# Moving the step sizes of a state-space mixer ahead of a branch, reordering its last group, and filling four waits with unread products

## What is computed

```python
def hgrn2_mixer(h, lb, w_in, o_norm, w_o):            # 8 heads
    ...
    o = rms_norm(o, o_norm) * gate
    return o.reshape(B, S, HV).astype(h.dtype) @ w_o

def ssd_mixer(z, xbc, dt, conv_w, conv_b, dt_bias, a_log, d_skip, norm_g):
    xbc = jax.nn.silu(causal_conv(xbc, conv_w, conv_b))
    ...
    dtc = jax.nn.softplus(dt.astype(jnp.float32) + dt_bias)   # 32 heads, in 4 groups of 8
    a = -jnp.exp(a_log)
    a_cum = jnp.cumsum(dtc * a, axis=2)                       # within chunks of 128 tokens
    ...
    y = rms_norm_2(y * jax.nn.silu(z), norm_g)

def second_block(x, ...):
    h = rms_norm_2(x, norm1_g[l])
    u = h @ w_in[l]                                           # dt is 32 of its columns
    ...
    mix = (gates[:, :, 0] * (y_a @ w_br_dsa[l]) + gates[:, :, 1] * (y_b @ w_br_nsa[l])
           + gates[:, :, 2] * (y_c @ w_br_ssd[l]))
    x = x + mix @ w_out[l]
    h = rms_norm_2(x, norm2_g[l])
    x = x + jnp.square(jax.nn.relu(h @ w_ff1[l])) @ w_ff2[l]
```

## Time and profile before

| | us |
|---|---|
| median of 3 runs | 2938.66 (2938.01 to 2939.58) |
| the profiled execution | 2933.7 |
| its span | 2931.9 |
| TensorE busy | 2760.3 (94%) |
| VectorE busy | 1620.9 (55%) |
| ScalarE busy | 1139.9 (39%) |
| GpSimd busy | 121.8 (4%) |

### The profile page before, as it was taken

How to read it: one execution, slowest core, us unless ns; L and a number is a source line. 1 busy time by engine, 2 the same in 40 slices (tenths; PEclk the granted TensorE clock), 3 DMA queues, 4 the chain that set the end, 5 groups by cost and what they waited for, 6 DMA issues and landing times.

```text
span 2931.9 us, 39152 instructions
## 1 busy us (share of the span) xinstructions
PE 2760.3 (94%) x14079; PEld 2226.9 (76%) x14079; DVE 1620.9 (55%) x3030; ACT 1139.9 (39%) x1896; POOL 121.8 (4%) x106
## 2 busy tenths in 40 slices
PE   7999999999999999998998998999899989999998
PEld 5567888888888788887675885667777767778887
DVE  6335726456554662645755347754677765464452
ACT  4344322236553422223437325842255543232221
POOL 0000000000000000000230001000011110000000
PEclk9999999999999999998999989999899999999999
DMA  4112333312111233232120220012222222333331
GB/s 142 38 58 72 115 93 94 100 44 79 57 57 36 79 115 93 94 100 65 58 72 1 87 70 18 1 56 81 74 70 72 65 65 72 115 101 101 93 100 65
DMA packets 59685, 217.83 MB, mean 74 GB/s; under 512 B 6433, under 2 KB 6561, under 8 KB 59425
## 3 DMA queue, kind: packets, MB, share of 16 engines
q1 hardware_dynamic: 57920, 209.76, 23.0%
q0 software_dynamic: 1632, 6.29, 0.6%
HBM read 211.83 MB, written 4.19 MB: 74 GB/s over the span
## 4 chain that ended last, share of the span: by engine, by line
PE 79%; DVE 11%; ACT 4%; issue 3%; DVEq 2%; ACTq 0%; DMA 0%; POOL 0%; SPq 0%
PE ps L366 22%; PE ps L368 22%; PE ps L367 22%; DVE work L2088 1%; PE ps L506 1%; DVE big L3176 1%; DVEq L3229 1%; DVE ring_lo L306 1%; PE ps L757 1%; PE ps L1558 1%; DVE work L2107 1%; PE ps L2014 1%; ACT ring_hi L299 1%; PE ps L1843 1%; PE ps L567 1%
## 5 line engine op out<-in xcount | busy, mean ns | idle before, releaser
L366 PE MATMUL ps<-a_hi,ring_hi 128*128 128x512 f32 (+1 forms) x1984 | 787.5, 397 | 45.1 <-DVE ring_lo L306 26.2
L368 PE MATMUL ps<-a_hi,ring_lo 128*128 128x512 f32 (+1 forms) x1984 | 772.7, 389 | 0.0
L367 PE MATMUL ps<-a_lo,ring_hi 128*128 128x512 f32 (+1 forms) x1920 | 746.2, 389 | 0.0
L306 DVE TENSOR_TENSOR ring_lo<-ring,ring_hi 128x1024 fp32r<-128x1024 f32 x358 | 437.9, 1225 | 518.5 <-ACT ring_hi L299 488.7
L299 ACT ACTIVATE ring_hi<-ring 128x1024 fp32r<-128x1024 f32 x378 | 397.6, 1055 | 507.9 <-PE ps L368 505.6
L366 PEld LDWEIGHTS ps<-a_hi,ring_hi 128*128 128x128 f32 x1984 | 379.8, 191 | 128.9 <-issue 21.3
L368 PEld LDWEIGHTS ps<-a_hi,ring_lo 128*128 128x128 f32 x1984 | 378.7, 191 | 77.7
L367 PEld LDWEIGHTS ps<-a_lo,ring_hi 128*128 128x128 f32 x1920 | 367.3, 191 | 71.2 <-issue 1.2
L367 PE MATMUL ps<-hid_lo,ring_hi 128*128 128x512 f32 (+1 forms) x992 | 381.1, 384 | 0.0
L366 PE MATMUL ps<-hid_hi,ring_hi 128*128 128x512 f32 (+1 forms) x928 | 354.6, 382 | 1.5 <-DVE ring_lo L306 1.5
L368 PE MATMUL ps<-hid_hi,ring_lo 128*128 128x512 f32 (+1 forms) x928 | 354.3, 382 | 0.0
(11 more groups left out here) (411 smaller groups left out, 3350.7 us busy)
## 6 DMA issues: line engine op xcount, KB each, us to landing
ring<-weights SPq DMA_DIRECT2D x392, 512.0 KB, 3.6
h<-x SPq DMA_DIRECT2D x1, 2048.0 KB, 9.5
residual<-h POOLq DMA_DIRECT2D x4, 512.0 KB, 3.5
h<-residual POOLq DMA_DIRECT2D x1, 2048.0 KB, 11.1
out<-h POOLq DMA_DIRECT2D x1, 2048.0 KB, 7.8
tab<-tables SPq DMA_DIRECT2D x1, 1648.0 KB, 15.8
big<-positions SPq DMA_DIRECT2D x1, 256.0 KB, 3.7
col<-columns SPq DMA_DIRECT2D x1, 164.5 KB, 3.9
```

The costliest lines, as they stand in the source:

```text
L306: dve.tensor_tensor(lo, M.ring[:, b % RING, :], hi.bitcast(F32), ALU.subtract).then_inc(M.sem("blocks_split"), 1)
L366: pe.matmul(out, w_hi, hi, start=start, stop=False)
L367: pe.matmul(out, w_hi, lo, start=False, stop=False)
L368: return pe.matmul(out, w_lo, hi, start=False, stop=stop)
```

## The change

1. `hgrn_pe`: `total` is called at k=6 instead of k=4.
2. `Pairs.pe`: six products that nobody reads between the first and the second scores.
3. dt gets a stage of its own, `ssd_dt`, one block, between the pairs of nsa and `nsa_out`. Its product goes to a PSUM bank of its own (`STEP_BANK`). VectorE's series is cut in four parts, one in each turn of `nsa_out`, between the first two rests and the first sum; ScalarE's exponentials stand before `nsa_out` and behind its first turn. The second block of `nsa_out` is rounded and its rest made among the splits of y. The loops of ScalarE and VectorE in `branch_out_*` are written out; TensorE's stays a loop. `ssd_pe` begins with `project(0, 0)`.
4. Last group of ssd: VectorE makes the last head's differences right after the ones before, and both last products with `cb` before the third pair's output; the rest of a block, two sums and the four `low` come behind. ScalarE has the last head's exponentials a step earlier. Four unread products stand before the last `output`, four at the start of `ssd_out_pe`.
5. `tail_pe`: the first two blocks of `mix_out` run over seven of eight steps as soon as `mix_split` has seven, then over the eighth; the other six follow.
6. The first block of `ff_up0` has places of its own (`first_hi`, `first_lo`) and is rounded and split during `mix_out`.

The same weights are loaded in the same number of blocks; nothing else is moved on SP's or GpSimd's queues.

```diff
-    ("nsa_in", 18), ("dsa_out", 8), ("nsa_out", 16),
-    ("ssd_in", 41), ("ssd_gate", 8), ("ssd_out", 16), ("mix_out", 8),
+    ("nsa_in", 18), ("dsa_out", 8), ("ssd_dt", 1), ("nsa_out", 16),
+    ("ssd_in", 40), ("ssd_gate", 8), ("ssd_out", 16), ("mix_out", 8),
...
+    if b == FIRST["ff_up0"]:
+        return M.first_hi[:, :], M.first_lo[:, :], RING
...
-            if k == 4 and between:
+            if k == (4 if j else 6) and between:
                 between()
...
         scores(0, 0)
+        idle_pe(pe, M, PIECE_BANK, 6)
         scores(0, 1)
...
-    with dve.Fori(0, NT // 2) as i:
+    for i in range(NT // 2):
         for u in range(2):
             rest_block(dve, M, FIRST[name] + u + 2, i, 4)
+        beside(i)
         for u in range(2):
             dve.wait_ge(M.sem("gates_ready"), i * 2 + (u + 1 + NT * BRANCHES.index(name)))
...
     R.pairs.pe(pe, M, compressed)
+
+    b = FIRST["ssd_dt"]
+    wait_split(pe, M, b)
+    for k in range(BLK):
+        mm = split_matmul(pe, M, M.bank(STEP_BANK), b, k, M.a_hi[:, k, :], M.a2_lo[:, k, :], k == 0, k == 7)
+    mm.then_inc(used, 1)
     branch_of_pairs_pe(pe, M, "nsa", NT)
...
-    branch_out_act(act, M, "nsa_out")
+    steps_logs_act(act, M, ssd)
+    round_block(act, M, FIRST["nsa_out"] + 1)
+    branch_out_act(act, M, "nsa_out", lambda i: steps_exp_act(act, M, ssd) if i == 0 else None)
...
-    branch_out_dve(dve, M, "nsa_out", lambda: split_y_dve(dve, M, "nsa", R.y))
+
+    def before():
+        split_y_dve(dve, M, "nsa", R.y, range(0, 5))
+        rest_block(dve, M, FIRST["nsa_out"] + 1)
+        split_y_dve(dve, M, "nsa", R.y, range(5, NT))
+
+    branch_out_dve(dve, M, "nsa_out", before, lambda i: steps_dve(dve, M, ssd, i))
...
     pe.wait_ge(M.sem("nsa_out_free"), NT + 2)
-    project(0, -1)
     for s in range(2):
         project(0, s)
...
             if s == 9:
+                if g + 1 == GRPS:
+                    idle_pe(pe, M, 0, 4)
                 output(g, 3)
...
     pe.wait_ge(M.sem("ssd_free"), SSD_READ + NT)
+    idle_pe(pe, M, 0, 4)
...
+def steps_dve(dve, M, R, part):
...
+    if part == 1:
+        dve.wait_ge(M.sem("small_done"), 6)
+        dve.tensor_scalar(t_, ab, 2.0, None, ALU.add)
+        dve.drain()
+        dve.reciprocal(s_, t_)
...
+        series((15, 13))
+    if part == 2:
+        series((11, 9, 7, 5, 3))
...
+    last = GRPS - 1
+    mix(last, 7)
+    segments(last, 7)
+    decay_cb(last, 6)
+    decay_cb(last, 7)
+    pair_out(last, 2)
+    rest_block(dve, M, FIRST["ssd_gate"] + NT + 1)
+    sums(7)
+    low(range(0, 4))
+    pair_out(last, 3)
+    sums(9)
...
-    pe.wait_ge(M.sem("ssd_out_free"), NT + 2)
+
+    pe.wait_ge(M.sem("ssd_out_free"), NT + 1)
+    pe.wait_ge(M.sem("mix_split"), NT - 1)
+    for u in range(2):
+        part_of_tile_pe(pe, M, "mix_out", u, M.in_hi, M.in_lo, range(0, NT - 1))
     pe.wait_ge(M.sem("mix_split"), NT)
-    gemm_split_pe(pe, M, "mix_out", NT, 1, lambda k: M.in_hi[:, k, :], lambda k: M.in_lo[:, k, :], 4)
+    for u in range(2):
+        part_of_tile_pe(pe, M, "mix_out", u, M.in_hi, M.in_lo, range(NT - 1, NT))
+    gemm_split_pe(pe, M, "mix_out", NT, 1, lambda k: M.in_hi[:, k, :], lambda k: M.in_lo[:, k, :], 4, done=2,
+                  looped=False)
...
+        else:
+            act.wait_ge(M.sem("blocks_used"), FIRST["mix_out"])
+            round_block(act, M, FIRST["ff_up0"], fresh=True)
         tile(t)
     act.wait_ge(M.sem("blocks_used"), FIRST["ff_up0"])
-    round_block(act, M, FIRST["ff_up0"], fresh=True)
     round_block(act, M, FIRST["ff_up0"] + 1, fresh=True)
```

More of the change, by code:

```diff
@@ L2124 @@
 BRANCHES = ["nsa_out", "ssd_out"]
+STEP_BANK = 4
 def branch_out_pe(pe, M, name, y_hi, y_lo, wait_y):
@@ L2143, in branch_out_pe, with branch_out_act @@
             mm.then_inc(used, 1)
-def branch_out_act(act, M, name):
-    with act.Fori(0, NT // 2) as i:
+def branch_out_act(act, M, name, behind):
+    for i in range(NT // 2):
         for u in range(2):
@@ L2154, in branch_out_act, with branch_out_dve @@
             round_block(act, M, FIRST[name] + u + 4, i, 4)
-def branch_out_dve(dve, M, name, before):
+        behind(i)
+def branch_out_dve(dve, M, name, before, beside):
     dve.drain().then_inc(M.sem(f"{name}_free"), 2)
     before()
-    with dve.Fori(0, NT // 2) as i:
+    for i in range(NT // 2):
         for u in range(2):
             rest_block(dve, M, FIRST[name] + u + 2, i, 4)
+        beside(i)
         for u in range(2):
@@ L3123, in ssd_act @@
         for s in range(STEPS):
-            if s != 1:
+            if s != 1 and not (g + 1 == GRPS and s == 8):
                 mix(g, s)
+            if g + 1 == GRPS and s == 7:
+                mix(g, 8)
             if g + 1 < GRPS:
@@ L3307, in ssd_dve @@
     for g in range(GRPS):
-        for s in range(STEPS):
+        for s in range(STEPS if g + 1 < GRPS else NT - 1):
             if s == 1:
@@ L3313, in ssd_dve @@
             if s == 9:
-                if g + 1 == GRPS:
-                    low(range(0, 4))
                 pair_out(g, 3)
@@ L3621, in lay_weights @@
     z, sx = w["sz"], w["sx"]
-    order = [wide(w["sdt"])]
+    put("ssd_dt", pack(wide(w["sdt"])))
+    order = []
     for g in range(GRPS):
```

157 lines of the change are left out of this document (79 added, 78 removed).

## The result

| | before | changed |
|---|---|---|
| median, us | 2939.12 (2938.01 to 2941.74, 4 runs) | 2896.29 (2895.42 to 2902.01, 4 runs) |
| profiled execution | 2933.7 | 2896.5 |
| its span | 2931.9 | 2894.7 |
| mean granted clock in it | 0.972 | 0.980 |

The ratio is 0.9857, interval 0.9840 to 0.9874; the change gains 42.8 us. The prediction was 2910.8 us, a gain of 27.9, with a range that began at 2901: right in sign, too small by a third, and the time lies outside the range. Between the two profiled executions the gain is 37.2 us.

A forecast was written before the change was run, and what follows sets the result against it. TensorE, busy 94% of the span, was taken to bound the kernel. 7.8 + 1.0 + 13.0 + 2.7 + 2.4 + 1.0 = 27.9 us off the 2938.66 median gave 2910.8 us, range 2901 to 2921.

The forecast's parts named there:

- the two new waits: Third turn of `nsa_out`, 3.0 us plus 1.6 of clock; `mix_out` before its third block, 2.0 us plus 1.4.
- the series: VectorE's step-size work inside `nsa_out`: hidden but for 3.0 us, where without cover it would cost some 17.
- the unread products of the last group: Before the last `output` and before `ssd_out`: worth nothing and costing nothing.
- the footing on the median: Whole kernel: the median of 2938.66 us is 5.0 above the profiled execution, and the gain was taken off that median.
- the heads: Recurrent heads: six waits of 1.30 us before the total go, 7.8 us; bounds 6.5 and 7.8.
- the pairs: Second scores in `Pairs.pe`: six idle products take 1.46 us and the clock falls later, 1.0 us; bounds 0 and 3.7.
- terms 5 and 6: `mix_out` begun early, 2.4 us (bounds 2.2 and 3.9); `ff_up0`'s first block rounded early, 1.0 us (0.8 and 2.4).
- Rival a: Pairs, `nsa_out`, `mix_out`, `ff_up0`: the clock stays at 2.4 GHz, together 7 us more won, 2904 us; chance 0.20.
- the bound of 3.7: Second scores in `Pairs.pe`: 2.2 + 1.5 us would go if the clock stood.
- Step sizes: `ssd_dt` moved ahead of `nsa_out`: 17.6 less 3.0 of waiting and 1.6 of clock, 13.0 us; bounds 11 and 16.
- Last group: Last group of ssd: the new order fills VectorE's own waits, 2.7 us; bounds 1.5 and 3.4.

The follow-up runs named there:

- run 4: The changed kernel with three calls of unread products in the pairs instead of six: 2896.49 us.
- Runs 1 and 2: The kernel before with one edit each: the heads' total at k=6 instead of k=4, 2924.79 us; two calls of unread products before each total's wait, 2928.84 us.
- run 9: The changed kernel itself once more, with no further edit: 2895.37 us, ratio 0.9860.

## Why the prediction was wrong

**The direction** was right: each of the six terms is a gain at its place, the two new waits came where forecast (2.27 us for 3.0, 1.88 for 2.0), the series is hidden but for 2.27 us, the unread products of the last group are worth nothing. The sum was too small by 14.9 us, and the steps that failed are, by size: the footing on the median (5.6), the heads, where the clock behind the waits was put at nothing (5.1), and the pairs, where the unread products were miscounted (3.6). The clock behind the two waits of terms 5 and 6 adds 2.4.

The likeliest case was not the one that came. Rival a, "the clock is kept", came for the pairs, `nsa_out` and `mix_out` and by less than half for `ff_up0`, and was itself too small: it said 2904. That it came owes something to luck. At the pairs it needed twelve passes and not the six of the prediction, after which the clock falls (run 4); and the same waits in `nsa_out` and before `mix_out`'s third block were followed by 1.2 GHz in the half-filled kernel.

**1. Heads, 12.9 instead of 7.8.** The failed step is "six waits of 1.30 us, so 7.8 us go". Only the waits were priced; the clock behind them stood at nothing, with no row for it. The nearest row was the gap of 1.81 us that isn't followed by the lower clock, and the granted clock of the heads was never asked for. Runs 1 and 2 show the missing 5.1 as three stretches of 1.7.

The Trainium skill, page "TensorE: Matmul & The Clock Gate", section "Why this matters for your kernels", warns only of gaps above some 3 us, and by it the heads had no second price. The trace disagrees: 1.2 GHz follows three of six waits of 1.30 us.

**2. Pairs, 4.6 instead of 1.0.** Two errors. The count: the row with x6 belongs to a call `idle_pe(..., 3)`, since every call is two passes, and so the price of a call was 0.24 us where it is 0.48. The call stood in the code beside the row. And the bound of 3.7 counted only the scores; the turns behind them had run at the lower clock too. With the stretch that still follows, the two uses had 10.2 us each at 1.2 GHz near these waits in before and have 3.4 each now.

**3. Step sizes, 13.4 instead of 13.0.** Right in sum, by parts that cancel: the gap is 0.7 shorter and had no slow restart (1.6), but the 1.2 GHz behind the mark before `nsa_out` cost 1.4 us more than in before, and the way from the end of `nsa_out` to the end of the third block of ssd is 23.2 us where the working gives 22.3. Some 0.4 us I can't place.

**4. Last group, 1.9 instead of 2.7.** At the start of `ssd_out` the lead over before has grown by 2.8 us, from 29.55 to 32.31, as said; 0.85 is given back behind it, in a longer stretch at the lower clock. VectorE's two products with `cb` beside GpSimd's took 2.80 us together, 1.4 more than alone where I took 0.7.

**5 and 6. 5.8 instead of 3.4.** Waits as forecast. Behind the 1.88 us of `mix_out` the clock did not fall (1.4 more). Behind the 2.31 us before `ff_up0` it did, as the prediction had it, but for 3.4 us instead of 5.7, which is the 1.0 more.

**The footing, 5.6 us.** The profiled execution of before took 2933.7 us, 5.0 below its median, and I let the changed kernel keep that distance. But 2933.7 was a lucky execution: beside run 9 the kernel before spans 2932.94 to 2941.58 with its clock, and in the changed kernel the profiled execution lies at the median (2896.5 and 2896.3). All upper bounds together, 37 us, are what the traces show, but that is a coincidence: the heads and the pairs went over their upper bounds (12.9 over 7.8, 4.6 over 3.7) and the step sizes and the last group stayed under theirs. Taken from the profile's own time the bounds give 2896.7, still 0.4 above the measured median; taken from the median they gave 2901.4, the end of my range. With the 5.1 us of clock in the heads as well the range would have held it. So the range failed by these two steps, and neither alone is clearly enough.

**What stays open.** What beside the length of a wait decides whether the clock falls. Counted over the fourteen traces, waits that began at full clock and that 1.2 GHz followed within 5 us:

| wait before a product, us | waits | followed by 1.2 GHz |
|---|---|---|
| 1.0 to 2.0 | 376 | 68 |
| 2.0 to 2.5 | 91 | 52 |
| 2.5 to 3.0 | 16 | 10 |
| 3.0 to 3.75 | 34 | 30 |
| 3.75 to 5.0 | 36 | 36 |

Other waits and narrow products close by are in these counts, and the traces share most of their lines, so these are not that many separate cases and no law; but none of the rows is all or nothing below 3.75 us, and I had used as if they were. In the heads one and the same wait at one line goes either way in turn, so neither length nor line decides it. Whether the moment at which a wait comes does was not tried.

## What to carry to other kernels

Read the granted clock of every stretch that a term touches, for some microseconds behind a wait and not at it, and price a wait together with the stretch that follows; where the waits are short, give that price a probability instead of a rule. When TensorE waits anyway, unread products that end before the wait does cost nothing and here bought 23 us without a change of order, but only where the work behind them is on the path, and the slow stretch can still come, shorter or later. Check a row's count against the call that made it, and take differences between two profiled executions only after asking how each lies among its kernel's own runs.
